# A decoder layer step on one core: attention order, output projection, expert loads and the layout of the expert rows are changed

## The reference

```
rq, rk, rv, rg, mq, mk, mv, ga, gb = split(x @ w_in)
o_r  = silu(rg) * (groupnorm(retention(rq, rk, rv)) * gn_g)      # 4 heads of 128
o_m  = block_sparse_attention(mq, mk, mv)                        # 8 heads of 64
y    = (sigmoid(ga) * (o_r @ w_br_ret) + sigmoid(gb) * (o_m @ w_br_moba)) @ w_out
x1   = layer_norm(ALPHA * x + y)
# router: best of 4 groups, then the best 2 of its 8 experts, weights e_w
moe  = sum over the 2 chosen experts of e_w * (silu(x1 @ w_eg) * (x1 @ w_eu)) @ w_ed
out  = layer_norm(ALPHA * x1 + moe)
```

## Time and profile before

| | us |
|---|---|
| three runs | 691.24, 693.68, 694.03 |
| median | 693.68 |
| profiled execution | 689.35 |
| its span in the profile | 687.5 |

### The profile page before, as it was taken

The page is one execution under the profiler, slowest core; times in us unless marked ns, Lnnn a source line. Parts: engine busy times, 40 slices in busy tenths (PEclk is TensorE's granted clock), DMA queues, the critical chain, the costliest instruction groups (busy, mean ns, idle before and its releaser), DMA issues.

```text
span 687.5 us, 10970 instructions
## 1 busy us (share of the span) xinstructions
PE 610.0 (89%) x4390; PEld 502.6 (73%) x4390; DVE 309.6 (45%) x602; ACT 143.4 (21%) x290; POOL 75.4 (11%) x78
## 2 busy tenths in 40 slices
PE   3999999999998798799999999999933999999863
PEld 2999999999975564699999998788732555554410
DVE  6344343444337568734445544464575122222126
ACT  0111011030155255310001112120111232322202
POOL 0101400021052000000000000000003122221114
PEclk9999999999998999989999999999955999999977
DMA  9425322136307435022333312595078799999195
GB/s 355 160 75 173 117 62 92 61 92 210 115 21 219 119 118 185 32 62 92 123 138 128 106 59 92 208 415 209 33 279 315 276 409 417 414 415 384 69 211 178
DMA packets 45977, 124.43 MB, mean 181 GB/s; under 512 B 6289, under 2 KB 19729, under 8 KB 41714
## 3 DMA queue, kind: packets, MB, share of 16 engines
q1 hardware_dynamic: 39888, 112.23, 46.1%
q0 software_dynamic: 4752, 8.93, 3.5%
q10 hardware_dynamic: 1298, 2.73, 1.0%
HBM read 114.62 MB, written 17.43 MB: 192 GB/s over the span
## 4 chain that ended last, share of the span: by engine, by line
PE 75%; DVE 8%; DMA 8%; issue 3%; ACT 3%; SPq 2%; POOLq 0%; DVEq 0%; ACTq 0%
PE ps L709 13%; PE ps L707 13%; PE ps L708 13%; PE ps L1035 6%; PE ps L702 6%; DMA scratch<-experts 3%; PE ps L1050 3%; DMA arena<-token_rows 3%; PE ps L926 2%; PE ps L983 2%; PE ps L928 2%; PE ps L927 2%; PE ps L985 2%; PE ps L984 2%; PE ps L769 1%
## 5 line engine op out<-in xcount | busy, mean ns | idle before, releaser
L707 PE MATMUL ps<-xa_hi,w_hi 128*128 128x272 f32 x704 | 205.8, 292 | 11.4 <-DVE xa_lo L1441 11.4
L709 PE MATMUL ps<-xa_hi,w_lo 128*128 128x272 f32 x704 | 204.4, 290 | 0.0
L708 PE MATMUL ps<-xa_lo,w_hi 128*128 128x272 f32 x704 | 203.8, 290 | 0.0
L707 PEld LDWEIGHTS ps<-xa_hi,w_hi 128*128 128x128 f32 x704 | 133.7, 190 | 12.7 <-issue 10.0
L708 PEld LDWEIGHTS ps<-xa_lo,w_hi 128*128 128x128 f32 x704 | 133.9, 190 | 0.0
L709 PEld LDWEIGHTS ps<-xa_hi,w_lo 128*128 128x128 f32 x704 | 133.6, 190 | 0.0
L1432 DVE CAST w_hi<-w_ring 128x1024 fp32r<-128x1024 f32 x52 | 37.9, 729 | 114.3 <-PE ps L709 85.0
L1434 DVE TENSOR_TENSOR w_lo<-w_ring,w_hi 128x1024 fp32r<-128x1024 f32 x52 | 65.7, 1263 | 1.8
L1035 PE MATMUL ps<-arena,work 128*64 128x256 f32 x384 | 49.7, 394 | 2.9 <-ACT work L1269 2.2
L1374 POOL DMA_INDIRECT work<-x_rows,idx_i x13 | 13.3, 1027 | 343.3 <-DVE idx_i L1814 312.9
L1035 PEld LDWEIGHTS ps<-arena,work 128*64 128x64 f32 x384 | 29.8, 141 | 17.6 <-ACT work L1269 2.9
(11 more groups left out here) (263 smaller groups left out, 874.6 us busy)
## 6 DMA issues: line engine op xcount, KB each, us to landing
w_ring<-w_tiles SPq DMA_DIRECT2D x52, 512.0 KB, 3.5
arena<-experts SPq DMA_DIRECT2D x24, 1024.0 KB, 13.9
arena<-experts SPq DMA_DIRECT2D x24, 512.0 KB, 16.9
arena<-kT_pool SPq DMA_DIRECT2D x16, 256.0 KB, 3.1
out<-arena SPq DMA_DIRECT2D x4, 1024.0 KB, 5.4
arena<-v_pool SPq DMA_DIRECT2D x16, 256.0 KB, 2.9
arena<-token_rows SPq DMA_DIRECT2D x8, 512.0 KB, 11.3
cst<-experts SPq DMA_DIRECT2D x3, 1024.0 KB, 23.0
```

The costliest lines, as they stand in the source:

```text
L707: mm(out, w_hi[b][:, w], x_hi[:, k_x, cols], start=start, stop=False)
L708: mm(out, w_hi[b][:, w], x_lo[:, k_x, cols], start=False, stop=False)
L709: return mm(out, w_lo[b][:, w], x_hi[:, k_x, cols], start=False, stop=stop)
```

## The change

1. **Decay at evacuation.** The group order ends with RQ, MQ. RQ leaves PSUM through DVE, which multiplies by a decay table (`qdec`, now 272 columns a head). POOL's four multiplies and the semaphore `s_qd` go.
2. **A new `ORDER`.** The two heads of a pair are turned apart (`turned_head`), with retention jobs between. `reto` products stand at other places. `std` and the split of weight tile 0 move behind the turns of head (3, 0). SP issues `key_pages(1)` ahead of `store_head(1)`.
3. **End of the attention.** ACT scales the 16 retention blocks (it was DVE), and makes `w_hi` of tiles 0 and 1. There is a third weight buffer (`w_hi2`, for tile 1). The five turns of the rows (new job kind X) go ahead of `pv(3)`, each with a PSUM bank of its own. Gate tile 1 comes right behind `pv(3)`.
4. **Output projection of token tile 0 in three parts** (`first_rows`): input blocks 0 to 3 ahead of the last branch tile, 4 to 6 and 7 behind it.
5. **Fillers** (`stay_active`): 17 matmuls of an identity ahead of the ranks, 17 ahead of the one-hots, 15 behind them. Nothing reads what they write.
6. **Twelve slots.** The twelfth lies where x1 of the first three token tiles lies. Experts 3 to 6 are loaded, then, when x1 is turned and stored, 7 and 11, all ahead of the first gather. x1 of three tiles and the second layer norm's scale and shift are loaded behind the twelfth expert pair. 20 refills are left.
7. **Rows side by side.** `token_rows` goes in blocks of 64 tokens: 64 rows of choice 0, then the same tokens' rows of choice 1. SP loads each block by one DMA of 128 partitions. DVE works out the row numbers with six more small instructions.

The core of the diff:

```diff
-SLOTS = 11
+SLOTS = 12
...
+        def turned_head(p, u):
+            return [("T", ("moba", p, u, kb)) for kb in range(4)]
+
         ORDER = ([("S", ("inner",))] + moba(0) + [("S", ("samp", 0))] + O("cross", 0) + inv(0) + skv(0)
-                 + [("R", ("samp", 0))] + turned(0)
-                 + moba(1) + ret(0) + O("pv", 0) + inv(1) + [("T", ("samp", 0))] + O("reto", 0)
-                 + ret(1) + O("sampv", 0) + turned(1) + O("sel", 0) + O("reto", 1)
-                 + moba(2) + ret(2) + O("pv", 1) + [("S", ("samp", 1))] + inv(2) + O("cross", 1)
-                 + O("reto", 2) + ret(3) + [("R", ("samp", 1))] + turned(2) + skv(1) + O("reto", 3)
-                 + moba(3) + O("pv", 2) + [("T", ("samp", 1)), ("N", ("std",)), ("W", (0,))] + inv(3) + O("sampv", 1)
-                 + [("N", ("rows",))] + turned(3) + O("sel", 1) + [("G", (0,))] + O("pv", 3))
+                 + [("R", ("samp", 0))] + turned_head(0, 0) + ret(0) + turned_head(0, 1)
+                 + moba(1) + O("pv", 0) + [("T", ("samp", 0))] + inv(1) + O("reto", 0) + O("sampv", 0) + ret(1)
+                 + turned_head(1, 0) + O("reto", 1) + turned_head(1, 1) + O("sel", 0)
+                 + moba(2) + O("pv", 1) + [("S", ("samp", 1))] + inv(2) + O("cross", 1) + ret(2) + [("R", ("samp", 1))]
+                 + skv(1) + turned_head(2, 0) + O("reto", 2) + turned_head(2, 1)
+                 + moba(3) + ret(3) + O("pv", 2) + [("T", ("samp", 1))] + inv(3) + O("reto", 3)
+                 + O("sampv", 1) + turned_head(3, 0) + [("N", ("std",)), ("W", (0,))]
+                 + turned_head(3, 1) + [("N", ("rows",)), ("W", (1,))] + O("sel", 1) + [("G", (0,))]
+                 + [("X", (t,)) for t in range(TT)] + O("pv", 3) + [("G", (1,))])
...
+        def w_buf(m):
+            return 2 if m == 1 else m % 2
+
+        def x_bank(t):
+            return (4, 5, 2, 3, 6 + (O_IDX[("pv", 3)] + 1) % 2)[t]
...
             sp.wait_ge(s_y, TT)
-            for s in range(3, 8):
+            for s in range(3, 7):
                 load_parts(s, experts_d[s])
-            sp.dma_start(ln_g, ln2_g.partition_broadcast(P)).then_inc(s_ln2, 16)
-            sp.dma_start(ln_b, ln2_b.partition_broadcast(P)).then_inc(s_ln2, 16)
+            sp.wait_ge(s_x1t, TT)
+            sp.wait_ge(s_x1s, 16 * TT)
+            for s in (7, 11):
+                load_parts(s, experts_d[s])
...
             refill_down(10)
+            sp.wait_ge(s_dn, 12)
+            sp.dma_start(x_tm[:, 0:3], x1_d[0:3 * P].rearrange("(t p) n -> p t n", p=P)).then_inc(s_x, 16)
+            sp.dma_start(ln_g, ln2_g.partition_broadcast(P)).then_inc(s_ln2, 16)
+            sp.dma_start(ln_b, ln2_b.partition_broadcast(P)).then_inc(s_ln2, 16)
...
             for t in range(TT):
-                r = P if t < 4 else NS
-                for c in range(2):
-                    rows = rows_d[c * T + t * P:c * T + t * P + r]
+                for g in range(2):
                     if t < 4:
-                        sp.dma_start(picked[c * CAP:(c + 1) * CAP, t], rows.rearrange("(g p) n -> p g n", g=2)
-                                     ).then_inc(s_yg[t], 16)
+                        at = (2 * t + g) * P
+                        sp.dma_start(picked[:, t, g], rows_d[at:at + P]).then_inc(s_yg[t], 16)
                     else:
-                        sp.dma_start(x_tm[(c + 1) * NS:(c + 2) * NS, t, :], rows).then_inc(s_yg[t], 16)
+                        at = 2 * NP + g * CAP
+                        sp.dma_start(x_tm[(g + 1) * NS:(g + 2) * NS, t, :], rows_d[at:at + NS]).then_inc(s_yg[t], 16)
...
-                if m < 2:
+                if m == 0:
                     pe.wait_ge(s_su, nS)
+                elif m == 1:
+                    pe.wait_ge(s_olo, TT)
                 else:
                     pe.wait_ge(s_cgs, 2 * n - 1 if kind == "a" else 2 * n)
...
+            def turn_rows(t):
+                pe.wait_ge(s_gn, t + 1)
+                if t < 2:
+                    pe.wait_ge(s_tu, nT)
+                elif t < 4:
+                    pe.wait_ge(s_su, nS)
+                else:
+                    pe.wait_ge(s_ou, done("sel", 1))
+                b = x_bank(t)
+                if t < 4:
+                    for c in range(4):
+                        m = tr(ps[:, b, c * P:(c + 1) * P], rg_t[:, t, c * P:(c + 1) * P], P)
+                else:
+                    m = tr(ps[:, b, 0:P], xs, P)
+                m.then_inc(s_ot, 1)
...
+            EARLY = ((0, 4), (4, 7), (7, KD))
+
+            def first_rows(part):
+                if part == 0:
+                    pe.wait_ge(s_cgs, 16)
+                pe.wait_ge(s_ml, part + 1)
...
+            for m in range(2, 3 * KD):
+                if m == 3 * KD - 1:
+                    first_rows(0)
...
+            first_rows(1)
+            first_rows(2).then_inc(s_y, 1)
...
+            def stay_active(n):
+                for _ in range(n):
+                    mm(ps[:, 3, 0:P], ident, ident, start=True, stop=True)
+
+            stay_active(17)
...
+            stay_active(17)
...
             m.then_inc(s_ohu, 1)
+            stay_active(15)
...
+            def scaled_rows():
+                act.wait_ge(s_gnm, 1)
+                for t in range(4):
+                    for h in range(RH):
+                        o = rk_t[:, t, h * P:(h + 1) * P]
+                        n = 4 * h + t
+                        m = A(o, o, ACT.Identity, scale=gstd[:, n:n + 1], bias=gmv[:, n, 0:1])
+                    m.then_inc(s_nr, 1)
...
+                    h, b = n - 20, 2 * (n % 2)
+                    q, decay = fm[:, 4 * FM_OF[RQ] + h, :], C("qdec")[:, h * HALF:(h + 1) * HALF]
+                    skip = HALF % P
+                    v.tensor_tensor(q[:, 0:HALF], ps[:, b, 0:HALF], decay, ALU.mult)
+                    v.tensor_tensor(q[:, HALF:NP], ps[:, b + 1, 0:NP - HALF], decay[:, skip:skip + NP - HALF], ALU.mult)
+                    v.tensor_copy(q[:, NP:T], ps[:, b + 1, NP - HALF:HALF]).then_inc(s_pev, 1)
...
+                v.scalar_tensor_tensor(gmv[:, 0:4 * RH, 0], gmv[:, 0:4 * RH, 0], -1.0, gstd[:, 0:4 * RH], ALU.mult, ALU.mult
+                                       ).then_inc(s_gnm, 1)
...
                 for t in range(4):
-                    for h in range(RH):
-                        o = rk_t[:, t, h * P:(h + 1) * P]
-                        n = 4 * h + t
-                        m = v.tensor_scalar(o, o, gmv[:, n, 0:1], gstd[:, n:n + 1], ALU.subtract, ALU.mult)
-                    ch.link(m)
+                    dve.wait_ge(s_nr, t + 1)
                     v.tensor_tensor(rg_t[:, t, :], rg_t[:, t, :], rk_t[:, t, :], ALU.mult).then_inc(s_gn, 1)
...
             def split_tile(m):
-                if m == 0:
-                    dve.wait_ge(s_o, max(done("reto", 3), done("cross", 1)))
-                    dve.wait_ge(s_s, used(("samp", 1)))
-                elif m == 1:
+                if m < 2:
+                    dve.wait_ge(s_hi, 28 + m + 1)
+                    v.tensor_tensor(w_lo[w_buf(m)][:], w_ring[:, m % 4, :], w_hi[w_buf(m)][:].bitcast(F32), ALU.subtract
+                                    ).then_inc(s_spl, 1)
+                    return
...
+            ts_(past_f, held, float(T - EMPTY), float(CAP), ALU.is_ge, ALU.mult)
+            L(v.tensor_copy(row_i[:], tok_f))
+            L(ts_(row_i[:], row_i[:], 6, None, ALU.logical_shift_right))
+            L(v.tensor_copy(sixty_f, row_i[:]))
+            L(v.scalar_tensor_tensor(row_f[:], sixty_f, float(CAP), tok_f, ALU.mult, ALU.add))
+            L(tt_(row_f[:], row_f[:], past_f, ALU.add))
+            L(v.scalar_tensor_tensor(row_f[0:1], C("iota", 1)[:, 0:COLS], float(ROW0), row_f[0:1], ALU.add, ALU.min))
             v.tensor_copy(row_i[:], row_f[:]).then_inc(s_row, 1)
```

190 lines of the change are left out of this document (94 added, 96 removed).

## The result

| | before | changed |
|---|---|---|
| runs (us) | 690.04, 691.24, 693.68, 694.03 | 664.11, 666.92, 667.58, 667.81 |
| median | 692.46 | **667.25** |
| profiled execution | 689.35 | 667.81 |
| its span | 687.5 | 666.0 |

The ratio is **0.963**, 95% interval 0.9585 to 0.9674: some 25 us faster. Stretches that no edit touches came out up to 3 us apart in the profiles that follow, so a difference of under 3 us between stages of two profiles says little, unless it lies between neighbouring events or comes back in several profiles. The runs of before are the three that were known and a fourth.

A forecast was written before the change was run, and what follows sets the result against it. PE was taken as the bound in most stretches, full DMA engines in routing and sum. Terms -10.0 - 1.7 - 0.5 - 3.2 - 7.2 = -22.6 took 689.35 to 666.8; 4.3 us to a median gave 671, range 658 to 685.

The forecast's parts named there:

- the clock stays up: Rival, chance 0.10: clock kept through the gather and behind the new ACT wait, head waits at their bound: 665.
- Attention, -10.0: Attention: POOL's decay -3.7, turned rows -5.6, order -3.2, new ACT wait +2.5; bounds -16 and -3.
- I take half: Attention, new order: half of the 6.5 us of remaining PE waits goes, -3.2; bounds 0 and -6.5.
- The new wait on ACT, +2.5: Attention: table load, root and cast between the copies of heads (3, 0) and (3, 1); from 0 to 3.9.
- ACT's 16 scalings, 4 us: Attention's end: ACT's block scalings take 2.1 to 5.1 us, lie beside gate tile 0, and add nothing.
- Projection, -1.7: Output projection: PE 3.3 us earlier, DVE some 6 us late; half taken, bounds -3.3 and 0.
- Fillers, -0.5: Routing: fillers cost nothing, speed only ranks and one-hots; first expert pair still starts low; were it otherwise, -3.0.
- Gather, +0.5: Ahead of the experts: 0.5 MB more loaded may delay the gather; bounds 0 and 1.3.
- Rows side by side, -7.2: The sum: 128-partition loads reach 389 GB/s instead of 221, DVE becomes the bound; ends 5.6 and 8.7 us gained.
- a slow load: Rival, chance 0.12: the sum's loads of rows stay slow, rate perhaps set by the 4 KB pieces: 678.
- an order that gives nothing: Rival, chance 0.20: ACT and DVE set the attention's head waits, so it gains only its bound of -3: 678.
- Slower: Rival, chance 0.05: the attention waits for ACT; sign turns with five more standstills of 4.5 us, six give 698.

The follow-up runs named there:

- the experiment: The changed kernel with the decay of the retention queries put back on POOL, PE waiting for it: 672.37 us, ratio 0.973.
- by halves: The changed kernel with each load of 128 rows cut into two loads of 64 partitions: 672.08 us, ratio 0.972.
- the three mends: The changed kernel with experts 7 and 11 behind the first gather, weight tile 0's cast earlier, root later, layer norm's wait at its reader: 659.98 us, ratio 0.9543.

## Why the prediction came out right

671.0 was predicted, 667.25 measured. The sum of -22.6 stands against -21.5 between the profiled executions (666.8 forecast, 667.81 measured). That the forecast is 3.75 us high comes from the 4.3 us that were added to bring it to a median: the profiled execution of the change was not under its median but the slowest of its four. By the number alone, 667.25 is nearer to the rival "the clock stays up" (665) than to the forecast; the trace parts them, since the first expert pair started low and the clock fell behind the new wait. And that the sum fits is in part luck: in the attention terms that were too small and terms that were too large cancel.

- *Attention, -10.0.* Right as a sum: 8.8 us off the stretch, and the low clock behind it gone (1.3 in the prediction). In its pieces it was off. From the end of gate tile 0 to gate tile 1, where the turned rows stand, 5.6 us went (4.3 predicted); up to gate tile 0 POOL and the order together, less the new wait, brought 5.1 (4.4 predicted); and gate tile 0 lost 1.9, which the sum had at nothing. POOL and the order were priced as two terms, 3.7 and 0.7. The experiments show them bound together: undoing POOL's part costs 5.4 us, undoing the order 4.2, together more than the whole stretch gained. A standstill also has another length in another run of things: the first head's four scalings took 3.62 us beside POOL before, 6.07 us in the experiment, and the second head's 2.27 us were left out of the prediction. Counted by undoing, the term mis-sized most is the order. "I take half" of 6.5 us held for the waits it named (5.0 - 2.2 + 0.7 = 3.5 us of these kinds are left, without the new one). But 6.5 was not what the old order costs once POOL is out of the way: with it the same kinds, and one for the group statistics, come to 10.6 us. Of the 4.1 us between, 2.3 are a wait for DVE's scalings that was thought to go with POOL, and 1.9 stood in the list of waits of before and were not counted:

```profile
PE ps L867 <- DVE gstat L1522: 1.9, 1, 1.9
```

- *The bounds.* The attention's bound of -3 doesn't come out of its terms: -3.7 - 5.6 + 3.9 is -5.4. Nor does the low end: its four pieces together are 11.6 us, which gives 659.4, not 658. Neither changes the outcome.
- *The new wait on ACT, +2.5.* There, 2.24 us long, at the place named, with the lower clock behind it that only the bound had included.
- *ACT's 16 scalings, 4 us.* They took 6.26, above the bound of 5.1 that came from DVE's rate. Gate tile 0 covered them, running at half clock for most of its length. In the run with the root behind the last head PE waited 2.4 us for the rows; there gate tile 0 ran at full clock, and the scalings also started 2.9 us later against it (1.8 us behind its first matmul, not 1.1 ahead), so the runs don't say which of the two uncovers them.
- *Projection, -1.7.* About right. DVE started 6 us behind y(0), as said, and PE's wait at x1(0) was 1.98 us.
- *Fillers, -0.5, and the clock.* The waits ahead of ranks and one-hots were filled, but nothing came of it, since the loads set the landing. The first pair started low, as the prediction took it by the trace. The Trainium skill's rule (TensorE: Matmul & The Clock Gate, section HAM oscillation) agreed here, behind a wait of 5.3 us. The page speaks of long stops; behind a wait of 1.6 and 1.7 us for the gather the first pair started at the upper clock.
- *Gather, +0.5.* The term outside its bounds: "0 and 1.3", measured +1.6 in spite of a gather issued 1.3 us earlier. By the other kernels with six experts and fillers it would be +0.7 to +1.2, so the excess is small. The larger transfer was the right cause. What was left out is that the gather also lands behind whatever is left of it, however early it is issued.
- *Last expert, -3.7.* -4.2; the wait and the low clock behind it are gone (1.00 from 620 to 636).
- *Rows side by side, -7.2.* -8.0. The rate was 410 to 416 GB/s, above the 389 taken, and DVE is the next bound, as said, with 2.95 us a tile. The Trainium skill, SBUF — State Buffer, section Door 1 (64 partitions reach half of the ports), agrees: 228 to 231 GB/s by halves.

Of the rivals, a slow load and an order that gives nothing are refuted. "Slower" would have needed five more standstills on ACT; there was one. "The clock stays up" was not the case in the change, and three of the experiments show that through the gather it can be. One sign was missed in part: DVE's four scalings take 1.28 us in the first head, but 1.88 in the second, beside POOL's other products.

## What to carry to other kernels

A load that is issued ahead of a gather delays it by what is left of its transfer, so before loading more ahead, see whether the gather's issue or the queue sets its landing: here two experts behind the gather instead of ahead were worth 6 us by the medians, 4.4 by the ratios to the kernel before. Cut a transfer so that each one spans all 128 partitions. Two causes that feed one wait can't be priced one by one: by these profiles POOL's work gone or the order changed alone, beside the rest of the change, gains 1.4 or 0.4 us ahead of gate tile 0, both together 5. And look where a gain goes: in the profile of the three mends the attention's was lost to waits for the rows and a lower clock, and a part of the gather's to late refills. The totals don't show this: by the medians the mends took 6, 3 and 3 us and together 7, by the ratios (times the 691 us of the kernel before) 4.4, 0.6 and 1.7 and together 6.0, and two of the three are not told apart from nothing.

## What the runs showed of the hardware that was not expected

- A DVE scaling of a 128x128 block by one factor for each partition, read from memory, lasted 5.08 us, through some seven of POOL's instructions (from the third of the four multiplies to the last of POOL's rows above), until POOL had none left; before, no scaling at this place took over 1.37 us, beside the same instructions of POOL. Why one was held through the row and the others not stays open. The Trainium skill, SBUF — State Buffer, section Who interferes with whom, has DVE and GpSimd share one pair of ports by an exclusive lock. The trace agrees that one blocks the other, and shows that the block can outlast the one instruction that holds it.
- Loads of 64 partitions, queued one behind the other for the two halves, moved 221 (two rows a partition) and 228 to 231 GB/s (one row) at a DMA share of 1.03 to 1.04. The share reads full at half the rate, so it does not show which of the two a shape gets; the GB/s do.
- ACT's scaling of a 128x128 block with a scale and a bias from memory took 0.39 us (6.26 / 16), though a cast of eight times the columns took 1.04.
